# Mixture-of-experts visits of two kinds: from two loops in sequence to one alternating loop

## What is computed

```python
def hier_moe(tokens, w1, b1, w2, b2, w_gate, w_up, w_down):
    ...
    top_val, top_idx = lax.top_k(lg2, TOP_K_INNER)
    gate = p_grp * jax.nn.softmax(top_val, axis=-1)
    expert = grp * EXPERTS_PER_GROUP_2 + top_idx
    return grouped_experts(tokens, expert, gate.astype(tokens.dtype), w_gate, w_up, w_down)

def grouped_experts(...):
    ...
    def run(args):
        xb, e = args
        return (jax.nn.silu(xb @ w_gate[e]) * (xb @ w_up[e])) @ w_down[e]
    ys = lax.map(run, (xs, block_e)).reshape(cap, d)
    return jnp.zeros((n + 1, d), x.dtype).at[slot_tok].add(ys * slot_w[:, None])[:n]
```

## Time and profile before

| | |
|---|---|
| median of three runs | 3375.06 us |
| the profiled execution | 3381.49 us |
| its span, first to last instruction | 3379.8 us |
| mean granted clock of PE | 0.897 of full |
| PE busy | 2632.9 us (78% of the span) |
| DVE, ACT, POOL busy | 871.4, 415.0, 279.9 us |
| moved by DMA | 744.57 MB, mean 220 GB/s |

### The profile page before, as it was taken

How to read it: one execution, slowest core, us unless ns; L and a number is a source line. 1 busy time by engine, 2 the same in 40 slices (tenths; PEclk the granted TensorE clock), 3 DMA queues, 4 the chain that set the end, 5 groups by cost and what they waited for, 6 DMA issues and landing times. The chain is left out here.

```text
span 3379.8 us, 34102 instructions
## 1 busy us (share of the span) xinstructions
PE 2632.9 (78%) x11124; PEld 1356.0 (40%) x11124; DVE 871.4 (26%) x1534; ACT 415.0 (12%) x779; POOL 279.9 (8%) x415
## 2 busy tenths in 40 slices
PE   6996779768985998867775999649699837777692
PEld 4431144234433553524432444225376424433240
DVE  1221253000004795410000000160357520000004
ACT  1011140000001001000000000010055100000000
POOL 3001140200001000020000000000000010000001
PEclk8998878898997998879997999869899959999796
DMA  9426611779954112279997899442001149999783
GB/s 345 135 78 222 210 13 57 292 315 343 335 218 142 50 50 77 75 279 421 423 423 305 323 333 338 166 137 75 0 13 36 33 177 418 423 423 422 273 296 118
DMA packets 150429, 744.57 MB, mean 220 GB/s; under 512 B 13552, under 2 KB 15264, under 8 KB 101168
## 3 DMA queue, kind: packets, MB, share of 16 engines
q1 hardware_dynamic: 100784, 592.46, 45.3%
q0 software_dynamic: 35568, 115.04, 9.9%
q10 hardware_dynamic: 13968, 35.66, 2.8%
HBM read 664.24 MB, written 79.46 MB: 220 GB/s over the span
## 5 line engine op out<-in xcount | busy, mean ns | idle before, releaser
L681 PE MATMUL ps<-w_ring,arena 128*64 128x256 f32 x3136 | 369.1, 390 | 133.3 <-DMA w_ring<-in_e_up 59.7
L604 PE MATMUL ps<-w_ring,arena 128*128 128x512 f32 x960 | 429.4, 602 | 7.2 <-ACT arena L600 7.2
L232 PE MATMUL ps<-x_feat,w_ring 128*128 128x512 f32 (+1 forms) x1152 | 421.5, 528 | 7.9 <-ACTq L145 3.7
L681 PEld LDWEIGHTS ps<-w_ring,arena 128*64 128x64 f32 x3136 | 221.5, 140 | 285.2 <-DMA w_ring<-in_e_gate 91.8
L232 PEld LDWEIGHTS ps<-x_feat,w_ring 128*128 128x128 f32 x1152 | 220.6, 192 | 208.0 <-issue 192.9
L604 PEld LDWEIGHTS ps<-w_ring,arena 128*128 128x128 f32 x960 | 183.3, 194 | 227.0 <-issue 222.5
L706 PE MATMUL ps<-w_ring,arena 128*64 128x512 f32 x784 | 182.3, 607 | 41.0 <-DMA w_ring<-in_e_down 35.4
L626 PE MATMUL ps<-w_ring,arena 128*128 128x512 f32 x480 | 211.3, 593 | 2.3 <-ACT arena L621 2.3
L324 PE MATMUL ps<-w_ring,x_feat 128*128 128x512 f32 x448 | 198.4, 606 | 13.7 <-ACTq L145 12.1
L955 PE MATMUL ps<-w_ring,fcol 128*2 128x512 f32 x384 | 182.0, 630 | 3.2 <-issue 2.3
L690 DVE TENSOR_TENSOR arena<-arena,ps 128x256 f32<-128x256 f32 x49 | 20.7, 421 | 629.9 <-PE ps L681 629.9
(11 more groups left out here) (272 smaller groups left out, 2326.9 us busy)
## 6 DMA issues: line engine op xcount, KB each, us to landing
w_ring<-in_e_gate SPq DMA_DIRECT2D x63, 2048.0 KB, 17.5
w_ring<-in_e_up SPq DMA_DIRECT2D x63, 2048.0 KB, 17.9
w_ring<-in_e_down SPq DMA_DIRECT2D x63, 2048.0 KB, 17.2
w_ring<-in_ada_w SPq DMA_DIRECT2D x24, 2048.0 KB, 10.2
w_ring<-in_w_gate SPq DMA_DIRECT2D x16, 2048.0 KB, 10.7
w_ring<-in_w_up SPq DMA_DIRECT2D x16, 2048.0 KB, 10.4
w_ring<-in_w_down SPq DMA_DIRECT2D x16, 2048.0 KB, 8.6
arena<-expert_rows ACTq DMA_DIRECT2D x39, 512.0 KB, 8.6
```

The lines of the kernel that those rows point to most:

```text
L232: mm = nc.tensor.matmul(pair(j)[:, t0:t1], w[:, k, c0:c0 + P], x_feat[:, k, t0:t1], start=k == 0, stop=k == KT - 1)
L604: mm = nc.tensor.matmul(bank(2 + part), blk_feat[:, s, k, :], chunk_view(slot, FF)[:, k, :], start=k == 0, stop=k == KT - 1)
L681: mm = nc.tensor.matmul(bank(2 + part)[self.H * c:self.H * (c + 1), 0:256], blk_feat[:, s, i, self.H * h:self.H * (h + 1)], w[:, h, i, 256 ...
```

## The change

It replaces the two loops per mixture and engine by one that does visit i of Singles and then visit i of Doubles in each iteration. The parts are:

- w_ring is used by the doubles alone; the singles get four slots of their own (small_slots) in x_feat, in rows and in the arena (A_TOK). Each kind has semaphores of its own for landed and freed slots.
- The buffers of a visit are single, one set per kind (blk_ and half_), not double; rows of visit i+2 are loaded in iteration i. PSUM bank 7 holds the singles' down product; banks 0 to 4 are shared by both kinds, so PE waits for the other kind's readers.
- The barrier between the kinds goes. SP issues both kinds' first gate and up before it waits for the scatter.
- used_visits gets a third entry, the larger of the two counts. A turn of four iterations of both kinds is passed by one condition when it is beyond that.
- The parameters of the combine stage are loaded to last_rows, since the singles' slots cover the old place.

The core of the diff, with the new loops of SP, PE, ACT, DVE and POOL (the two classes lose the buffer number s in each method, and are else unchanged):

```diff
-        self.chunks = 3 * (self.doubles + self.singles) + 4
+        self.turns = max(self.doubles, self.singles) // 4
...
+        small_slots = [x_feat.rearrange("p k n -> p (k n)")[:, 0:SLOT], region(A_ROWS, SLOT), region(A_TOK, SLOT),
+                       region(A_TOK + SLOT, SLOT)]
...
+            v.tensor_tensor(used_visits[0:1, 2:3], ends[0:1, 0, E - 1:E], ends[0:1, 1, E - 1:E], ALU.max)
...
+            for kind in kinds:
+                for slot, (part, w) in enumerate((("gate", gate), ("up", up))):
+                    matrix = source(kind, w, 0, part)
+                    if kind.kind == "double":
+                        sp.wait_ge(w_free, chunks.n - 1 - (chunks.n - 1 - slot) % RING + 1)
+                    load(kind, slot, matrix)
+            sp.wait_ge(w_free, chunks.n)
+            sp.wait_ge(*count(f"{name}.scattered", 32 * m.T))
+            with sp.Fori(0, m.turns) as turn:
...
+                with sp.If(turn * 4 < n_most):
+                    for b in range(4):
+                        i = turn * 4 + (b + 1)
+                        for n, kind in enumerate(kinds):
+                            at = 3 * b + 2
+                            with sp.If(i < n_used[n]):
+                                for k, (part, w) in enumerate((("gate", gate), ("up", up))):
+                                    matrix = source(kind, w, i, part)
+                                    freed(kind, at + k - 1)
+                                    load(kind, (at + k) % 4, matrix)
+                            with sp.Else():
+                                for k in range(2):
+                                    freed(kind, at + k - 1)
+                                    sp.sem_inc(summed[f"{name}.{kind.kind}.landed{(at + k) % 4}"], 16)
+                            with sp.If(i < n_used[n] + 1):
+                                matrix = source(kind, down, i - 1, "down")
+                                freed(kind, at + 1)
+                                load(kind, (at + 2) % 4, matrix)
...
+                with sp.Else():
+                    for kind in kinds:
+                        freed(kind, 4)
+                        for slot in range(4):
+                            sp.sem_inc(summed[f"{name}.{kind.kind}.landed{slot}"], 48)
...
+            with pe.Fori(0, m.turns) as turn:
+                with pe.If(turn * 4 < n_most):
+                    for b in range(4):
+                        i = turn * 4 + (b + 1)
                         for n in range(2):
+                            other = 1 - n
+                            with pe.If(i < n_used[n]):
+                                pe.wait_ge(*count(at(n, "feat"), i + 1))
+                                pe.wait_ge(*count(at(other, "silu"), i + n))
+                                gate_or_up(n, 0, 3 * b + 2, turn)
+                                turn_hidden(n, i)
+                                pe.wait_ge(*count(at(other, "hid"), i + n))
+                                gate_or_up(n, 1, 3 * b + 3, turn)
+                                pe.wait_ge(*count(at(other, "feat"), i + 1 + n))
+                                turn_rows(n, i + 1)
+                                down(n, i, 3 * b + 4, turn)
+                            with pe.Else():
+                                pe.drain().then_inc(summed[at(n, "free")], 2)
+                                pe.sem_inc(summed[at(n, "turned")], 1)
+                                with pe.If(i < n_used[n] + 1):
+                                    turn_hidden(n, i)
+                                    down(n, i, 3 * b + 4, turn)
+                                with pe.Else():
+                                    pe.sem_inc(summed[at(n, "free")], 1)
+                                    pe.sem_inc(summed[at(n, "hid_turned")], 1)
+                with pe.Else():
+                    for n in range(2):
+                        pe.drain().then_inc(summed[at(n, "free")], 12)
+                        pe.sem_inc(summed[at(n, "turned")], 4)
+                        pe.sem_inc(summed[at(n, "hid_turned")], 4)
...
+                            with act.If(i < n_used[n]):
+                                act.wait_ge(summed[at(n, "free")], turn * 12 + (3 * b + 5 + start[at(n, "free")]))
+                                act.wait_ge(*count(at(n, "hid"), i))
+                                silu(n)
+                                take_hidden(n, i)
+                                take_features(n, i + 1)
+                                load_rows(n, i + 2)
...
+                            with dve.If(i < n_used[n]):
+                                freed(n, turn * 12 + (3 * b + 6))
+                                hidden(n, i)
+                                freed(n, turn * 12 + (3 * b + 7))
+                                outputs(n, i)
...
+                            with pool.If(i < n_used[n]):
+                                pool.wait_ge(*count(at(n, "y_copied"), i + 2))
+                                kinds[n].store(pool, i, first[n], summed[at(n, "stored")])
+                                pool.wait_ge(*count(at(n, "stored"), (i + 1) * kinds[n].stored))
+                                pool.sem_inc(summed[at(n, "out_free")], 1)
...
-            moe_blocks_pe(pe, "moe1", Singles(MOE1), chunks)
-            stage(pe, "pe", "singles1")
-            moe_blocks_pe(pe, "moe1", Doubles(MOE1), chunks)
+            moe_blocks_pe(pe, "moe1", MOE1)
```

More of the change, by code:

```diff
@@ L398, in moe_sems @@
                 shared(name, route_counts(m))
-                for kind, n in (("single", m.singles), ("double", m.doubles)):
-                    shared(f"{name}.{kind}", visit_counts(n))
+                for kind in ("double", "single"):
+                    for part, total in visit_counts(4 * m.turns).items():
+                        shared(name, {f"{kind}.{part}": total})
                     new_sems(f"{name}.{kind}", "stored")
@@ new lines, in moe_sp, with source, load @@
+            kinds = (Singles(m), Doubles(m))
+            n_used = [kind.used(sp) for kind in kinds]
+            n_most = most_visits(sp, m)
+            def source(kind, w, visit, part):
+                e = sp.value_load(expert_of[0:1, bass.ds(visit + kind.table_at, 1)], min_val=0, max_val=m.E - 1)
+                return kind.weights(w, e, part)
+            def load(kind, slot, source):
+                dest = kind.slot(slot)
+                if len(source.shape) == 3:
+                    dest = dest.rearrange("p (h n) -> p h n", h=2)
+                sp.dma_start(dest, source).then_inc(summed[f"{name}.{kind.kind}.landed{slot}"], 16)
```

531 lines of the change are left out of this document (249 added, 282 removed).

## The result

The changed kernel took 3287.89 us (median of four, 3275.07 to 3291.43), the kernel before beside it 3374.86: ratio 0.9739, 95% interval 0.971 to 0.9768. It is faster, by 87 us and not by 190; the time lies outside the range of 3150 to 3245. The profiled execution took 3275.07 us, 106.4 less than that of before.

The account below looks back on a forecast made before the run. Singles were taken as bound by DMA, doubles by PE, one after the other. Terms -80.9 - 11.3 - 109 - 5 + 11 + 5 = -190 us took 3375.06 to 3185 us; range 3150 to 3245, 8 in 10.

Parts of the forecast that it names:

- rival 1: Merged loop's code is fetched again each turn, 9 of 14 turns exposed at 5 us: 45 us, 3230; chance 0.19.
- E: Stage starts: both kinds' first weights issued before the scatter lands delay PE by 3, 5 and 3 us: +11.
- D: Idle turns: +5 us among stage 1's doubles running alone, -5 each at the ends of stages 2 and 3; net -5.
- The pair: One single and one double overlapped take 33.8 us at PE's pace; 38.1 without gain from overlap.
- rival 2: Pairs do not overlap and stay at 38.1 us: 112 us lost over 26 pairs, 3297; chance 0.11.
- F: Pairs near the DMA limit, where SP's one queue can let DMA run dry: +5 us over stage 2's 14 pairs.
- A to C: Hole between singles and doubles goes, -80.9 us; doubles' cold start goes, -11.3; singles run at PE's pace, -109.
- A: Hole between singles and doubles goes; the first double's turning products stay, about 2 us a stage: net -80.9 us.
- G: Single instead of double buffers for rows, features, hidden and outputs: 16.1 us of notice against 7.5 to land, cost 0.
- rival 4: Rows' landing exposed by single buffers on 79 visits at 7.5 us: 592 us slower, 3777; chance 0.01.
- Rivals 3 and 5: 3: code fetch stalls PE on each of 79 visits, 3580, chance 0.03. 5: gaps only move, about 3375, chance 0.02.

Follow-up runs that it names:

- e_shift_all: Changed kernel, its loops untouched, with never-run transposes ahead of stage 1's loop (74) and stage 3's (97): 3214.86 us, ratio 0.9525.
- e_split: Changed kernel with each turn choosing one of three bodies: both kinds, singles alone, doubles alone: 3354.41 us, ratio 0.9937.
- e_pass: Kernel before plus only the condition that passes four idle turns' visits at once, on each engine: 3346.18 us, ratio 0.992.
- e_lean_pad: Changed kernel with hidden transposes and down products written once per visit, plus 130 never-run transposes in each turn: 3300.73 us, ratio 0.9777.
- e_lean_pad60: Same as e_lean_pad but with 60 never-run transposes in each turn instead of 130: 3221.60 us, ratio 0.9553.
- e_shift: Changed kernel, its loops untouched, with 74 never-run transposes (150 instructions) ahead of stage 1's loop: 3247.96 us, ratio 0.9633.
- e_pad_spread: Kernel before with never-run transposes ahead of each visit in TensorE's loops (95 for singles, 115 for doubles): 3650.42 us, ratio 1.0836.
- e_shift_whole: Changed kernel, its loops untouched, with 127 never-run transposes (256 instructions) ahead of stage 1's loop: 3284.07 us, ratio 0.9732.
- e_pad: Kernel before with one lump of never-run transposes at the head of each TensorE turn (380 singles, 460 doubles): 3396.07 us, ratio 1.0065.

## Why the prediction was wrong in size

The step that failed is that the sum put the fetching of TensorE's code at nothing: it stood outside the sum, as rival 1. There its mechanism, its sign on q8 and its 14 turns were right; but it was put at 0.19 and priced at 9 x 5 = 45 us. What was held against it, that the trace has only smaller loops, was true, and the trace of before could not have told: 908 and 728 instructions are four and three pieces, together some 1640, and only the runs show where the limit lies. Two assumptions in the price were wrong. First, that a fetch beside DMA-bound singles hides (14 turns became 9): the lonely turns of singles were the worst. PE stops for 11.8 us in each, against 1.8 in a turn of pairs. Some of it is made up, since weights land meanwhile: two lonely turns take 70.8 and 70.9 us in the changed kernel and 63.9 each in e_shift_all, so 7.0 stay. Second, that a turn misses once: all seven or eight pieces are read again. The changed kernel against e_shift_all has 9.9, 18.0 and 34.9 us a stage, 62.8 in all by the profiles. Stage 3, where four of six turn rounds are lonely, has more than half of it: 4 x 7.0 = 28 of its 34.9.

Why lonely turns cost more is partly argued. In a turn of pairs PE runs straight through the code for 136 us, and one packet every 20 us can arrive ahead of it; in a lonely turn it jumps over the other kind's code and reaches each piece sooner. e_split's longer jumps make all three kinds of turn round worse, which fits; no run varied the jump alone.

Point by point, with the code's fetching taken out (e_shift_all: gains of 32.9, 81.1 and 49.6 us, 163.6 together, where 190 were forecast; 100.8 + 62.8 = 163.6, and the other 26 of the missing 89 stand in E and D below):

*The pair.* Right: 34.1 us against 33.8. The bound of no overlap (38.1) and rival 2 are out; PE is busy for all of 690 to 819 us, at 419 GB/s, in e_shift_all, and stage 2's pairs take 34.1 there too. F's 5 us stand, 14 x 0.3 = 4.

*A to C.* Right as far as the runs tell them apart. Lonely singles return to 16 us per visit as expected: 185 us with 23 of DVE's operations, two per visit, are 16.1. Lonely doubles take 23.8 us in e_shift_all, forecast 22.0 + 1.3:

```profile
885.55 7.13 PE L623 MATMUL ps<-w_ring,arena 128*128 128x512 f32 x16 [1.44 <-issue]
909.33 7.13 PE L623 MATMUL ps<-w_ring,arena 128*128 128x512 f32 x16 [1.57 <-issue]
```

*E, the start.* Mis-sized. 3, 5 and 3 us were taken, with 2 more for the transposes in A: 17 in all, and it was 8.0, 15.1 and 14.6, 38 in all. The bound of 10 a stage counted the doubles' weights, but not that the doubles' first transposes stand ahead of the singles' first product and wait for their own rows. In the changed kernel, stage 3:

```profile
2696.85 1.13 PE L689 MATMUL ps<-cst,arena 128*128 128x128 f32 x4 [57.49 <-DMA arena<-expert_rows]
2700.64 1.94 PE L614 MATMUL ps<-cst,arena 128*128 128x128 f32 x8 [2.66 <-DMA arena<-expert_rows]
2702.51 4.43 PE L701 MATMUL ps<-x_feat,arena 128*64 128x256 f32 x32
```

A DMA wait of 2.7 us, after the singles' own rows had come later as well.

*D, the ends.* Mis-sized. From the last product to the gather 9.6, 9 and 9 us were forecast; it was 11.5, 14.1 and 12.9, 11 more. In stages 2 and 3 that is what the ten idle visits had cost before. Passing idle turns does bring what was forecast in the old loops (9.1, 9.5 and 8.5 in e_pass); what the merged loop adds to it was not looked for by a run. E and D together are 32 us, the rest of the sum came out 5 better than forecast: that closes it to 164.

*G, single buffers.* Right: no transpose inside a loop waited for its rows, so rival 4 and the rule against single buffers did not bite here. Rivals 3 and 5 are out too: no fetch on each visit, and a gain.

What the Trainium skill says of code (Runtime: NRT & Kernel Launch, Instruction fetch mechanics), that PE holds 2048 instructions, would have let a loop of 1667 stay. The runs decide: 1515 and less was always kept, 1637 and 1667 were kept or not by where they begin. If a piece is 256 instructions, as q8's counts show, it is consistent with room for seven whole pieces and not eight.

The second count makes this sharper. Take pieces of 256 from the program's start, and ask where each loop ends within the seventh piece that it touches. In the kernels measured here every loop that was kept ends 81 instructions or more ahead of the end of that piece: 81 in stage 2 of e_lean_pad, 92 and more in the loops of e_lean_pad60, e_shift and e_shift_all that were kept and in stage 1 of e_pad_spread, which fits that this stage lost nothing. Every loop that was fetched ends 59 or fewer ahead of it (17 to 26 in stages 1 and 2 of the changed kernel and of e_shift_whole, 52 and 53 in stages 1 and 3 of e_lean_pad, 59 in stage 3 of e_shift) or beyond it. Only e_pad, whose lump is jumped over, is kept against this rule.

What stays open: why the edge lies 60 to 80 instructions ahead of the piece's end. Some code may stand ahead of the first that was counted, or the next piece may be fetched as well. That the place decides is shown (150 and 196 change it, 256 does not); the reason for the edge is not. Nor were single buffers tried against double ones in one kernel: there is no room for both with four matrices per kind.

## What to carry to other kernels

When a change merges loops, count the engine's instructions in the new loop before counting what it saves, and compare the packets of the instruction queue before and after: above the size of the program they mean code read again, and "issue" idle time at turn rounds is its price. Write each body once, under a condition of its own, rather than once per branch; near the limit a loop's place decided some 60 us here, so a change elsewhere in the program can bring or take them. An engine that waits for DMA hid the idle visits beside it, but only part of a stop for its own code: of 11.8 us 7.0 stayed, and DMA moved 375 GB/s in such a turn against 427. That it fell because PE gave slots back late is argued, not tested.

## What the runs showed that was not expected

- q8 carries TensorE's code in packets of 256 instructions: 63 packets for 16,128 instructions, 59 for 15,298, 64 for 16,526.
- A loop over the limit is read again whole, not in part: stage 1 of the changed kernel moved 28 packets against 8 in e_shift_all, 20 more with three turn rounds; 48 to 55 came in the six turns of stage 3.
- Reading a turn's code again cost 21 to 24 us when nothing ran beside it (e_pad_spread), 7.0 us net of an 11.8 us stop in lonely singles, and 1.8 us in a turn of pairs.
- Dead code in one lump inside a loop is nearly free of refetching (74 packets), in four pieces it is not (281), and ahead of a loop it made this kernel some 70 us faster.
- The granted clock was 0.88 in the lonely singles of the changed kernel (2945 to 3190 us), with holes of 12 us in PE, and 0.99 in those of e_shift_all (2945 to 3130).
